# Low halves of nine up-projection panels per layer made by a negated copy and an accumulating transfer

## The reference

```python
def first_block(x, ...):
    for l in range(DEPTH):                      # DEPTH = 2
        h = rmsnorm(x, attn_norm_w[l])
        proj = h @ w_in[l]
        ...
        x = x + jnp.concatenate([y_ssd, y_sc, y_nsa], axis=-1) @ w_out[l]
        h = rmsnorm(x, ffn_norm_w[l])
        u = causal_dwconv(h @ ffn_w_up[l], ffn_conv_w[l], ffn_conv_b[l])   # [1024, 2 x 2752]
        gate, val = jnp.split(u, 2, axis=-1)
        x = x + (jax.nn.silu(gate) * val) @ ffn_w_down[l]
    return rmsnorm(x, final_norm_w)
```

## Time and profile before

| | us |
|---|---|
| median of 3 runs | 2292.59 (2291.66 to 2293.55) |
| profiled execution, span from the first to the last instruction | 2290.5 |
| median less that span (what lies around it, and the difference of executions) | 2.1 |
| PE busy in the profiled execution | 2266.0 (99%) |
| DVE busy | 1699.2 (74%) |
| ACT busy | 950.0 (41%) |
| POOL busy | 119.7 (5%) |
| share of the DMA engines' time that the loads took | 44.3% |

### The profile page before, as it was taken

The page is one execution under the profiler, slowest core; times in us unless marked ns, Lnnn a source line. Parts: engine busy times, 40 slices in busy tenths (PEclk is TensorE's granted clock), DMA queues, the critical chain, the costliest instruction groups (busy, mean ns, idle before and its releaser), DMA issues.

```text
span 2290.5 us, 35253 instructions
## 1 busy us (share of the span) xinstructions
PE 2266.0 (99%) x14406; PEld 2012.7 (88%) x14406; DVE 1699.2 (74%) x2772; ACT 950.0 (41%) x1414; POOL 119.7 (5%) x85
## 2 busy tenths in 40 slices
PE   9999999999999999999999999999999999999998
PEld 8899999899998888898789888888888888989997
DVE  7989888989889858854446983884884673797774
ACT  6766545766542122235553212223321222475443
POOL 0010010200000000010001000001000001001001
PEclk9999999999999999999999999999999999999999
DMA  7355475354646545532111553553454453304543
GB/s 277 135 190 186 161 256 194 120 203 173 201 143 204 186 144 193 181 114 83 40 72 56 203 195 107 184 179 115 157 192 157 139 178 105 137 31 148 184 157 120
DMA packets 67025, 355.08 MB, mean 155 GB/s; under 512 B 7344, under 2 KB 10544, under 8 KB 43056
## 3 DMA queue, kind: packets, MB, share of 16 engines
q1 hardware_dynamic: 66304, 352.49, 44.3%
q10 hardware_dynamic: 560, 0.33, 0.0%
HBM read 351.75 MB, written 1.05 MB: 154 GB/s over the span
## 4 chain that ended last, share of the span: by engine, by line
PE 91%; DVE 6%; ACT 2%; issue 1%; DMA 0%; DVEq 0%; ACTq 0%
PE bank L555 90%; DVE sb_w_lo L2255 2%; ACT sb_w_hi L1486 1%; PE bank L1438 1%; DVE sb_products L2289 1%; ACT sb_nP L1486 0%; PE bank L1312 0%; DVE sb_nP L2951 0%; DVE sb_nP L2978 0%; DMA sb_res<-x 0%; DVE sb_mid L2859 0%; DVE sb_latP L3115 0%; DVE sb_decays L2990 0%; ACT sb_decays L1486 0%; DVE sb_mid L2860 0%
## 5 line engine op out<-in xcount | busy, mean ns | idle before, releaser
L1486 ACT ACTIVATE sb_w_hi<-sb_raw 128x2048 fp32r<-128x2048 f32 (+5 forms) x301 | 491.3, 1634 | 398.8 <-PE bank L555 394.4
L2255 DVE TENSOR_TENSOR sb_w_lo<-sb_raw,sb_w_hi 128x2048 fp32r<-128x2048 f32 (+3 forms) x280 | 564.1, 2015 | 117.8 <-ACT sb_w_hi L1486 114.0
L555 PE MATMUL bank<-sb_f_pair,sb_w_hi 128*128 128x256 f32 (+1 forms) x2090 | 523.9, 339 | 5.2 <-DVE sb_w_lo L2255 4.2
L555 PE MATMUL bank<-sb_h_hi,sb_w_hi 128*128 128x512 f32 (+1 forms) x1400 | 510.8, 365 | 0.6 <-DVE sb_w_lo L2255 0.4
L555 PE MATMUL bank<-sb_h_lo,sb_w_hi 128*128 128x512 f32 (+1 forms) x1400 | 507.3, 362 | 0.0
L555 PE MATMUL bank<-sb_h_hi,sb_w_lo 128*128 128x512 f32 (+1 forms) x1400 | 507.2, 362 | 0.0
L555 PEld LDWEIGHTS bank<-sb_f_pair,sb_w_hi 128*128 128x128 f32 x2090 | 360.3, 190 | 51.7 <-DVE sb_w_lo L2255 7.2
L2289 DVE CUSTOM_DVE_ANT_0 sb_products<-sb_raw,sb_cond,sb_params 128x1024 f32<-128x1024 f32 x280 | 360.0, 1286 | 32.9 <-DVEq L2291 16.2
L555 PE MATMUL bank<-sb_f_pair,sb_w_lo 128*128 128x256 f32 (+1 forms) x1122 | 366.1, 326 | 0.0
L555 PEld LDWEIGHTS bank<-sb_h_hi,sb_w_hi 128*128 128x128 f32 x1400 | 264.1, 189 | 42.9 <-issue 0.9
L555 PEld LDWEIGHTS bank<-sb_h_lo,sb_w_hi 128*128 128x128 f32 x1400 | 264.2, 189 | 41.2 <-issue 0.5
(11 more groups left out here) (329 smaller groups left out, 2917.0 us busy)
## 6 DMA issues: line engine op xcount, KB each, us to landing
sb_raw<-w_mod SPq DMA_DIRECT2D x144, 512.0 KB, 3.2
sb_raw<-w_l_up SPq DMA_DIRECT2D x44, 1024.0 KB, 4.8
sb_raw<-w_l_in SPq DMA_DIRECT2D x22, 1024.0 KB, 5.5
sb_raw<-w_l_down SPq DMA_DIRECT2D x32, 704.0 KB, 4.4
sb_raw<-w_m0a_up SPq DMA_DIRECT2D x22, 1024.0 KB, 4.8
sb_raw<-w_m0b_up SPq DMA_DIRECT2D x22, 1024.0 KB, 4.8
sb_raw<-w_m1a_up SPq DMA_DIRECT2D x22, 1024.0 KB, 4.8
sb_raw<-w_m1b_up SPq DMA_DIRECT2D x22, 1024.0 KB, 4.8
```

What stands on the lines that cost most here:

```text
L555: return nc.tensor.matmul(out, lhsT, rhs, start=start, stop=stop, skip_group_check=True)
L1486: return nc.scalar.activation(out, in_, func, **kw)
L2255: V.tensor_tensor(split_part(*at, w_lo[s]), landed_part(*at, raw[raw_slot(*at)]), split_part(*at, w_hi[s]).bitcast(F32), ALU.subtract).the ...
```

## The change

In each of the two layers, for the odd panels 3, 5, ... 19 of the up projection (nine of 22), DVE's subtraction is left out. In its place:
- ACT, in `tile(n)` after the two scaled copies, writes minus the rounded weights of panel n+3 into its low buffer (`opposite`, a copy with scale -1, 128x2048). It waits for the panel to have landed and for the buffer to be free.
- GpSimd waits for that and issues a DMA from the raw buffer onto the low buffer that adds (`accum_op=ALU.add`), so raw - high is left there (`low_begin`).
- GpSimd waits for the transfer to land, for the panel's high half and for the panels ahead, and raises `raw_free` (`low_end`). PE's and SP's waits are as before.

Panels 3, 7, 11, 15 and 19 get a low buffer of their own, `spare_lo` (8 KB per partition in a region that is free at that time); 5, 9, 13 and 17 keep `w_lo` of the odd slot. In the second layer GpSimd's additions for the context norm are put between the issues and the waits of panels 17 and 19.

```diff
+ADDED_LOWS = range(3, FF1_TILES - 1, 2)
+
+def low_is_added(name, n):
+
+    return name in FF1_UP and n in ADDED_LOWS
...
+        spare_lo = sb("spare_lo", [P, PANEL], F32R, at=H + 8192)
...
+            def low_begin(l, n):
+                name, i = FF1_UP[l], len(ADDED_LOWS) * l + ADDED_LOWS.index(n) + 1
+                pool.wait_ge(S("opposite"), i)
+                nc.gpsimd.dma_start(lo_buffer(name, n)[:, :], raw[raw_slot(name, n)][:, :],
+                                    accum_op=ALU.add).then_inc(S("low_added"), 16)
+
+            def low_end(l, n):
+                name, i = FF1_UP[l], len(ADDED_LOWS) * l + ADDED_LOWS.index(n) + 1
+                pool.wait_ge(S("low_added"), 16 * i)
+                pool.wait_ge(S("high"), SPLIT_AT[name, n] + 1)
+                pool.wait_ge(S("raw_free"), RAW_AT[name, n] + RAW)
+                pool.sem_inc(S("raw_free"), 1)
...
+                if i == 2:
+                    added_lows(0, 3, FF1_TILES - 1)
+                if i == 5:
+                    added_lows(1, 3, 17)
+                    low_begin(1, 17)
...
+                def opposite(n):
+                    act.wait_ge(S("panels_used"), SPLIT_AT[name + "_up", n] - 3)
+                    slot = raw_slot(name + "_up", n)
+                    act.wait_ge(S(f"landed{slot}"), landed_value(name + "_up", n))
+                    run(lo_buffer(name + "_up", n)[:, :], raw[slot][:, :], ACT.Copy, scale=-1.0).then_inc(S("opposite"), 1)
...
                     last.then_inc(S("conv_begun"), 1)
+                    if low_is_added(name + "_up", n + 3):
+                        opposite(n + 3)
                     if n:
                         mid_high(n - 1)
...
                         if n + 2 < count:
-                            low(name, n + 2)
+                            if not low_is_added(name, n + 2):
+                                low(name, n + 2)
```

More of the change, by code:

```diff
@@ L423, in raw_of, with lo_buffer @@
             return [x[:, k, :] for x in raw_in]
+        def lo_buffer(name, n):
+            if low_is_added(name, n) and n % 4 == 3:
+                return spare_lo
+            return w_lo[half_slot(name, n)]
         def hidden(half, N):
@@ L532, in mixed_lows, with added_lows @@
                                             ALU.subtract).then_inc(S("mixed_apart"), 1)
+            def low_begin(l, n):
[9 more added lines that the diff above has]
+                pool.sem_inc(S("raw_free"), 1)
+            def added_lows(l, first, end):
+                for n in range(first, end, 2):
+                    low_begin(l, n)
+                    low_end(l, n)
             squares_at, added = 0, 0
             for i, (squares, adds, a, b) in enumerate(NORMS):
-                for k in range(1, adds + 1):
+                if i == 2:
[3 more added lines that the diff above has]
+                    low_begin(1, 17)
+                for k in range(1, adds + 1):
+                    if i == 5 and k == 3:
+                        low_end(1, 17)
+                        low_begin(1, 19)
+                    if i == 5 and k == 5:
+                        low_end(1, 19)
                     pool.wait_ge(S("norm_sq"), squares_at + k + 1)
@@ L572, in panel @@
                 pe.wait_ge(S("raw_free"), RAW_AT[raws_of(name, n)[-1]] + 1 + RAW)
-                slot = half_slot(name, n)
-                return w_hi[slot], w_lo[slot]
+                return w_hi[half_slot(name, n)], lo_buffer(name, n)
             def panel_part(name, n, k):
```

## The result

The changed kernel takes 2345.51 us (median of 4 runs, 2341.9 to 2354.52) against 2292.43 for the one before (2291.66 to 2293.55): 53 us slower, ratio 1.0235, 95% interval 1.022 to 1.0249. Forecast were 2318.0 and a range of 2291 to 2345; the time lies just outside it, and the loss is twice the forecast one.

The account below looks back on a forecast made before the run. PE alone was taken to bound the up projections; landing in 8.8 us against 6.26 makes ten panels 2.54 us late, 25.4 us. Span 2290.5 + 25.4 = 2315.9, plus 2.1 gives 2318.0 us; range 2291 to 2345.

Parts of the forecast that it names:

- What bounds the stage: Up projections: PE alone bounds them, nobody waits for DVE, so removing its 41 us of subtractions gains 0.
- ACT's copies at 0: Eighteen negated copies of 1.92 us on ACT, covered by 1.40 us idle time; the next high half is not late.
- Budget of 6.26 us: Time from the end of ACT's negated copy to PE's need of that odd panel, within which the transfer must land.
- The five panels that pay: Panels 3, 7, 11, 15, 19 of each layer make PE wait 2.54 us each, ten in all, 25.4 us; others 0.
- Fixed part and second read (1.85 + 5.9 = 7.75): Adding transfer's landing time: 1.85 us fixed, plus 2 x 2.95 = 5.9 us for reading source and destination.
- The overlap with loads, 1.05 us: Delay of the transfer by the load SP issues 0.86 us ahead: half of at most 2.1 us.
- The rival of the slow transfer: Adding runs below copy rate or GpSimd's issue is slow: landing 11.2 us and over, 49.4 us lost, 2342; chance 0.16.
- A: Time from issue to landing of GpSimd's accumulating transfer; forecast 8.8 us, own range 7 to 11.

Follow-up runs that it names:

- e1: Changed kernel with only panels 7, 11, 15, 19 by transfer, negated copy one panel sooner (behind panel n-4): 2292.71 us, against 2293.84 for the kernel before.
- e4: Kernel before plus six 1 MB GpSimd transfers per layer onto an unused tile, adding in first layer, plain in second, no stage engine waiting: 2292.46 us.
- e2: Changed kernel with only panels 3, 7, 11, 15, 19 of each layer by transfer, five instead of nine: 2350.12 us.
- e6: Changed kernel with only panels 5, 9, 13, 17 of each layer by transfer, same lead and buffer: 2337.88 us.
- e9: Kernel before plus five GpSimd transfers, adding or plain, full or half width, in a last-attention stretch with hardly any load: 2294.78 us.
- e7: Changed kernel with negated copy and adding transfer covering columns 0 to 1023 only, DVE subtracting the others: 2326.94 us.
- e10: Kernel before, no transfer, but PE waits ahead of panels 3, 7, 11, 15, 19 for two GpSimd fills of an unused tile: 2354.16 us.
- e3: Changed kernel plus 34 filler matmuls on PE ahead of its wait for panels 3, 7, 11, 15, 19: 2351.31 us.
- e5: Changed kernel with five transfers per layer (panels 3, 7, 11, 15, 19) and 24 filler matmuls ahead of each wait: 2335.43 us.

## Why the prediction was wrong

- **What bounds the stage: right.** PE is bound by itself there. e1 and e4 show that neither DVE's relief nor the transfers move the time. DVE's 34 us fewer bought nothing.
- **ACT's copies at 0: right** for eight of them (e1, the same time as before); each took 1.90 us. PE's waits for ACT's high halves are 0.9 us in the whole changed kernel, 1.9 before.
- **Budget of 6.26 us: right up to 0.4.** Two steps were left out of it, 0.32 us from the copy's end to GpSimd's issue and 0.12 from the landing to PE. Ten times that is 4 us.
- **The five panels that pay: right** (e2, e6).
- **Fixed part and second read (1.85 + 5.9 = 7.75): right.** Alone such a transfer lands in 7.8 us (e9). Its parts are 5.4 of engine time, twice the plain one's 2.6 (e4), and the rest. What the Trainium skill says of an accumulate, that it reads its destination ("DMA: Bandwidth & Descriptors", section "Rules for kernel authors") agrees with that doubling. The fit of the same page, 4.4 us for a panel, agrees with the plain transfer alone (4.7) and not with the adding one.
- **The overlap with loads, 1.05 us: wrong.** The transfers into `spare_lo` landed in 10.0 us on the mean of ten (8.9 to 11.6), those into `w_lo` in 12.0 on the mean of eight (10.8 to 13.9). That is 2.2 and 4.2 above 7.8, where I had halved my own upper bound of 2.1. The halving had the transfer share the engines with the load ahead; e7's stretches show that it waits for that load. In stretches of 0.5 us, the transfers into `spare_lo` began to move 2.5 us after their issue on the mean (alone 1.0), and loads took 0.5 us of the engines' time while they moved; those into `w_lo` began after 3.5 us, and loads took 2.2 us within them. For the second part I had no term: the raw buffers that GpSimd frees late make the next loads come two at a time (at 164.06 and 166.46), one ahead of the next transfer and one into it. For the paying ones it is (10.0 - 8.8) x 10 = 12 us.
- **What the forecast had no term for: the clock.** 23.1 us in the profiled execution, over a third of the loss. e10 shows it with no transfer in the program, e3 and e5 show most of it gone (4.3 and 6.9 us left) when PE is kept busy. The earlier trace rows have the clock at 1.00, and I left it so for the new kernel, though it was that of a PE without gaps.

Together, for the profiled execution: 25.4 forecast + 4 + 12 + 23 = 64, against 62.2 measured; the first three, 42, stand for the 39.7 of idle time. The median of the runs lost 53; the four runs differ by 12.6 us, those of before by 1.9. The two slower ones had a mean granted clock of 0.987 and 0.989, the two faster ones 0.992 and 0.991; but longer waits would lower it too, so whether landing times or the clock make them differ is not shown.

The rival of the slow transfer had an A of 11.2 and 2342 us, close to the result, but by another way: it put the extra time into the adding itself. A was 11.2 by the median of all; of the ten that pay it was 10.0.

Left open: whether a transfer could be issued so that it falls between two loads. It would have to land within 6.26 us, and alone it takes 7.8, so with this lead it could not fit; that was not tried. No version beats the kernel before: the best one (e1) is equal to it.

## What to carry to other kernels

Work taken from an engine for which nobody waits is worth nothing, and what replaces it is worth minus its wait: look at the chain of the stage first, and then put the new path's latency, with every hand-over and with the loads ahead in the same DMA engines, against the time between its input and its use. Where TensorE runs without gaps, price a new wait of 3 to 6 us at the wait plus some 2.5 us, since the clock halves in it or just behind it and comes back only some us after work has begun again. Dummy matmuls in the wait kept most of the clock in both runs that had them; they gained time in e5, where no second transfer stands behind, and none in e3. A transfer that is to be used soon needs a lead of a panel more (e1), not fewer bytes (e7).

## What the runs showed of the hardware that was not expected

- PE's granted clock goes from 1.00 to 0.50 around the end of a wait of 3.8 us (e10) and is back 2.9 to 5.8 us after PE has resumed: 2.6 us lost on the mean. It also fell behind waits that were shorter, then only after PE had resumed: 0.7 us after in the changed kernel (2.25 us of idle), about 1 us after in e5 (2.7 us). In these runs it fell at every wait for GpSimd of 2.7 us and over, and at some between 1.8 and 2.5 us: 2.0 us brought it down in e2 at one place, 2.4 us in e7 (PE resuming at 243.07) did not.
- An adding transfer takes twice the engine time of a plain one of the same size (5.4 and 2.6 us for 1 MB), and lands alone in 7.8 against 4.7 us. A load of that size from HBM lands in 4.8.
- A GpSimd transfer issued just behind a load began to move only when that load was nearly done (4.6 us after issue in e7), although it is in another queue. A load issued after the transfer took about a third of the engines while both moved (32.4% against 62.8% and 70.7%). The Trainium skill ("DMA: Bandwidth & Descriptors", "Issuing engines are not separate DMA queues") says that such transfers interleave on the same engines; the trace agrees for the load behind, and hardly for the load ahead.
